# Hybrid layer with retrieved experts on one core: gathers of four choices of 32 tokens, 128x32 products, and another order of the head

## The reference

```
mod = silu(c) @ w_ada + b_ada                  # shift1, scale1, gate1, shift2, scale2, gate2
h = rms_norm(x, g_norm1) * (1 + scale1) + shift1
a, u, v = split(h @ w_in)                      # three times 512 columns
mixed = concat(pool_mixer(a), u * spatial(layer_norm(v)))   # windows of 2..16; 128-token chunks
x = x + gate1 * (mixed @ w_out)
h = rms_norm(x, g_norm2) * (1 + scale2) + shift2
q = h @ w_query                                # 8 heads x 2 sides x 128
scores = q . sub_keys                          # 128 keys a side
s_top, i_top = top_k(scores, 16)               # each side
best, sel = top_k(s_top0[:, None] + s_top1[None, :], 16)
idx = 128 * i0 + i1                            # one of 16384 experts
gate = softmax(best)
act = gelu(expert_down[idx] . h)
x = x + gate2 * sum(gate * act * expert_up[idx])
out = rms_norm(x, g_final)
```

## Time and profile before

| | us |
|---|---|
| median of 3 runs | 2961.24 (2958.83 to 2965.78) |
| the profiled execution's own time | 2958.65 |
| its span, first to last instruction | 2956.9 |
| TensorE busy | 2140.7 (72%) |
| VectorE busy | 1882.0 (64%) |
| ScalarE busy | 1144.8 (39%) |
| POOL busy | 1117.3 (38%) |
| moved by DMA | 1158.09 MB, mean 392 GB/s |
| mean granted TensorE clock | 0.797 of full speed |

### The profile page before, as it was taken

The page is one execution under the profiler, slowest core; times in us unless marked ns, Lnnn a source line. Parts: engine busy times, 40 slices in busy tenths (PEclk is TensorE's granted clock), DMA queues, the critical chain, the costliest instruction groups (busy, mean ns, idle before and its releaser), DMA issues.

```text
span 2956.9 us, 35079 instructions
## 1 busy us (share of the span) xinstructions
PE 2140.7 (72%) x12226; PEld 790.5 (27%) x12226; DVE 1882.0 (64%) x4560; ACT 1144.8 (39%) x3504; POOL 1117.3 (38%) x1029
## 2 busy tenths in 40 slices
PE   4587797888977767776767777777666677767665
PEld 3353352343523222221122222222111222222210
DVE  3846655665565666666676666666666666666664
ACT  1124335354352334433343434343343434343333
POOL 0013333343332444433444444434444444444432
PEclk9698898998978687877687677777777777777776
DMA  9459999999999999999999999999999999999997
GB/s 404 161 195 384 348 356 409 373 410 386 348 399 368 410 421 421 421 410 421 421 416 421 411 419 409 422 408 421 420 407 421 409 420 405 421 411 419 421 421 299
DMA packets 162730, 1158.09 MB, mean 392 GB/s; under 512 B 18164, under 2 KB 18932, under 8 KB 28024
## 3 DMA queue, kind: packets, MB, share of 16 engines
q0 software_dynamic: 147456, 1073.81, 88.9%
q1 hardware_dynamic: 15096, 82.04, 7.2%
HBM read 1147.38 MB, written 8.39 MB: 391 GB/s over the span
## 4 chain that ended last, share of the span: by engine, by line
DMA 47%; PE 30%; DVE 11%; ACT 7%; issue 3%; POOL 1%; SPq 0%; DVEq 0%; ACTq 0%; POOLq 0%
DMA weights<-experts,expert_rows 25%; DMA work<-experts,expert_rows 22%; PE ps_sum L635 13%; PE ps_q L606 6%; PE ps_m L577 3%; DVE work L1099 3%; DVE weights L1099 3%; PE ps_m L524 2%; PE ps_m L546 2%; PE ps_m L537 2%; ACT diag L800 2%; ACT weight L795 1%; POOL work L464 1%; DVE wide L875 1%; ACT act_out L793 1%
## 5 line engine op out<-in xcount | busy, mean ns | idle before, releaser
L635 PE MATMUL ps_sum<-work,diag 64*64 64x512 f32 x6656 | 1176.0, 792 | 534.9 <-ACT diag L800 532.3
L1099 DVE CUSTOM_DVE_ANT_0 work<-work,h_cur 128x1024 f32<-128x1024 f32 x832 | 1017.6, 1224 | 712.0 <-DMA work<-experts,expert_rows 710.2
L464 POOL DMA_INDIRECT work<-experts,expert_rows x832 | 893.8, 1074 | 1474.7 <-PE ps_sum L635 1263.8
L793 ACT ACTIVATE act_out<-act_in 128x1 f32<-128x1 f32 x1024 | 207.3, 202 | 1346.2 <-DVE act_in L1099 1345.5
L635 PEld LDWEIGHTS ps_sum<-work,diag 64*64 64x64 f32 x6656 | 210.7, 158 | 1339.9 <-ACT diag L800 1273.5
L635 PE MATMUL ps_sum<-weights,diag 64*64 64x512 f32 x1536 | 308.4, 886 | 186.4 <-ACT diag L800 177.3
L800 ACT ACTIVATE diag<-const,weight 128x64 f32<-128x64 f32 x1024 | 356.0, 348 | 33.5
L464 POOL DMA_INDIRECT weights<-experts,expert_rows x192 | 223.1, 1162 | 334.3 <-PE ps_sum L635 321.2
L1099 DVE CUSTOM_DVE_ANT_0 weights<-weights,h_cur 128x1024 f32<-128x1024 f32 x192 | 234.8, 1223 | 147.5 <-DMA weights<-experts,expert_rows 147.5
L795 ACT ACTIVATE weight<-gate,act_out 128x1 f32<-128x1 f32 x1024 | 301.8, 295 | 33.2
L606 PEld LDWEIGHTS ps_q<-h_t,weights 128*128 128x128 f32 x1152 | 144.0, 203 | 69.3 <-issue 69.3
(11 more groups left out here) (149 smaller groups left out, 1390.1 us busy)
## 6 DMA issues: line engine op xcount, KB each, us to landing
work<-w_ada SPq DMA_DIRECT2D x12, 2048.0 KB, 15.2
work<-w_query SPq DMA_DIRECT2D x7, 2048.0 KB, 11.5
work<-experts,expert_rows POOLq DMA_INDIRECT x832, 15.3
weights<-w_in SPq DMA_DIRECT2D x3, 2048.0 KB, 16.8
weights<-w_query SPq DMA_DIRECT2D x3, 2048.0 KB, 18.1
x_buf<-x SPq DMA_DIRECT2D x8, 512.0 KB
weights<-w_out SPq DMA_DIRECT2D x2, 2048.0 KB, 31.3
x_scratch<-h_buf SPq DMA_DIRECT2D x8, 512.0 KB, 3.0
```

The source lines that it names most:

```text
L464: nc.gpsimd.indirect_dma_start(ring[r], None, experts, bass.IndirectOffsetOnAxis(ap=expert_rows[:, g % SLOTS:g % SLOTS + 1], axis=0),).the ...
L635: last = nc.tensor.matmul(ps_sum[n * ROWS:(n + 1) * ROWS, r, :], diag[rows, slot, :], ring[slot][rows, D + n * HALF:D + (n + 1) * HALF], s ...
L793: nc.scalar.activation(act_out[:, s:s + 1], act_in[:, s:s + 1], ACT.Gelu).then_inc(s_gelu, 1)
L1099: nc.vector.tensor_tensor_reduce(down, down, h2_cur[:, :], 1.0, 0.0, ALU.mult, ALU.add, act_in[:, g % TURN:g % TURN + 1]).then_inc(s_dots, 1)
```

## The change

**The gather.** A gather still fetches 128 rows of 8 KB, but they are four choices of 32 tokens, where they were one choice of 128 tokens. All four quarters of the partitions then belong to the same 32 tokens. `diag` is 128x32, and `add_expert` makes four products of 128x32, each streaming 256 columns. The tokens' `h2` must stand four times below each other for the dots: `spread_h2` (a product of 32 rows by 128x512, two a segment) and `copy_spread` on ScalarE do that for each segment of 8 slots (tile 0) or 16 slots (from tile 1), 72 segments in all. The choices must be moved to their partitions: a 19th route step, four small products (`move_choices`) and two copies (`place_choices`) a turn. `y`, `x1_fin`, `gate2` and `gf` are in quarters too, so `load_x1_final` and `store_out` move rows of 1 KB, 32 partitions at a time, four transfers where there were two.

**The weights of the queries.** They come in sides (a side is half a head, 128 partitions of 4608 bytes, 0.59 MB, query and key weights together) in a buffer of two. Tiles 0 to 2 stream every side; from tile 3 on three turns of four find theirs held in SBUF (12 sides, loaded at slot 257), and the first turn's four sides are streamed in each tile. `LOAD_OF` has 66 sides; with 2 that go to ring slots at first and the 12 held, 80 sides are loaded.

**The mixer's steps.** There are 35 steps, with the U and out projections cut into twice as many pieces. Tile 1's mixer has 22 of its steps in slots 0 to 21, where 7 of 31 were.

**The head.** GATE1's sum stands ahead of tile 0's layer norm; tile 0's out projection runs on unscaled `w_out` and VectorE multiplies the result by gate1; `w_out` is scaled after the first route. The bias rows are put into the sums' tiles at first, so no row is added at the end. The first query is done side by side.

The core of the diff:

```diff
+QUADS = 4
+QROWS = P // QUADS
...
-MIX_AT = {1: -MIX_HEAD, 2: 12, 3: 48, 4: 93, 5: SLOTS + 4, 6: SLOTS + 40, 7: SLOTS + 85}
...
+MIX_AT = {1: -MIX_HEAD, 2: 25, 3: 64, 4: 103, 5: 142, 6: 181, 7: 220}
...
+BATCHES = [((0,), (1,), (2,), (3,))] + [((0, 1), (2, 3))] * (TILES - 1)
...
+def streamed(e):
+
+    return e // PAIRS <= MIX_TILES or e % PAIRS == 0
...
+            def load_side(e, b):
+                n = LOAD_OF[e, b]
+                if n >= 2:
+                    before = [key for key, m in LOAD_OF.items() if m == n - 2][0]
+                    sp.wait_ge(s_score, 4 * before[0] + before[1] + 1)
+                sp.dma_start(side_buf[n % 2], sides[4 * (e % PAIRS) + b]).then_inc(s_side[n % 2], 16)
...
-                for n in range(2):
-                    sp.dma_start(x1_fin[n * ROWS:(n + 1) * ROWS, :, :], x1_rows[t, n]).then_inc(s_x1f, 16)
...
+                for c in range(QUADS):
+                    sp.dma_start(x1_fin[quarter(c), :, :], x1_rows[t, c]).then_inc(s_x1f, 16)
...
+            def spread_h2(k, half):
...
+                pe.wait_ge(s_wide_sb, use)
+                nc.tensor.matmul(ps_wide[:, :], quads[quarter(group), :],
+                                 source[quarter(group), half * HALF:(half + 1) * HALF],
+                                 start=True, stop=True).then_inc(s_wide_ps, 1)
...
+            def add_expert(x):
...
+                for c in range(QUADS):
+                    last = nc.tensor.matmul(ps_sum[quarter(c), x.group, :], diag[:, x.ring, :],
+                                            ring[x.ring][:, D + c * QCOLS:D + (c + 1) * QCOLS],
+                                            start=x.first, stop=x.last, skip_group_check=True)
                 last.then_inc(s_free, 1)
...
             norm2(0)
-            mixer(2, 1)
+            mixer(FACTOR1, 1)
             sum_ada(GATE2)
             for n in range(ROUTE_STEPS):
-                route_step(n, 0, 0)
-            for n in (13, 16, 21, 22, 23):
-                mixer(n, 1)
```

More of the change, by code:

```diff
@@ L387, in _ @@
[L387 to L388 removed]
+            sp.wait_ge(s_zero, 3)
+            for m in (GATE1, SHIFT2, SCALE2):
+                sp.dma_start(totals[m][0:1, :], b_ada[m * D:(m + 1) * D].unsqueeze(0)).then_inc(s_b_ada, 16)
             load_ada(GATE1, 0)
@@ new lines, in _ @@
+            mod_rows(SCALE2)
+            turn_h2(0, 0)
+            turn_h2(0, 1)
+            side(0, 0)
+            side(0, 1)
+            for b in range(4):
+                scores(0, b)
+                if b < 2:
+                    side(0, b + 2)
+            spread_h2(0, 0)
+            spread_h2(0, 1)
+            mixer(TURN_H, 1)
+            mod_rows(GATE2)
+            move_choices(0)
+            for b in range(4):
+                side(1, b)
+                scores(1, b)
+            for n in range(TURN_H + 1, MIX_HEAD):
+                mixer(n, 1)
```

1136 lines of the change are left out of this document (628 added, 508 removed).

## The result

The changed kernel takes 2978.97 us, median of 6 runs (2973.78 to 2988.84); the kernel before took 2959.80 in the 6 runs beside it. The ratio is 1.0070, 95% interval 1.0048 to 1.0091: slower by 0.7%. The prediction said 2973, within 2938 to 3006. The profiled execution took 2976.63 us with a span of 2974.8, so 17.9 us more span than before.

What follows compares the result with a forecast made beforehand. The kernel was taken as a DMA transfer of 1158.09 MB at 421 GB/s plus 206 us of unused bandwidth. Terms +56 + 18 - 16 - 47 + 1 gave +12 us: 2973, range 2938 to 3006.

Steps and rivals of the forecast that it cites:

- Item 1: Query and key weights: 80 sides, 47.2 MB, replace 23.6 MB, so 23.6 MB more at 421 GB/s, +56 us.
- Item 2: Reads of x1 in 1 KB rows: cost goes by the row, +18 us after slot 256 and +6 before.
- The stated bound of 0: Other bound for the x1 reads: the halved rows cost nothing.
- rival A: Faster: quarter reads of x1 are free, the dip coming from something other than row length; 2949 us, chance 0.25.
- Item 3: Head, to 225 us: unused bandwidth falls from 89 to 73 us, first refill at about 193.5; -16 us.
- Item 4: Tiles 0 and 1: unused bandwidth falls from 75 to 28 us, -47 us, the 6 for x1 reads included.
- Item 5: Later tiles keep their 33 us unused, plus 18 for x1 reads; spreads and moves lie beside; tail +1 us.
- rival C: Slower: the four 128x32 products do not run together, about 120 us more TensorE time, 3090 us; chance 0.04.
- D: Slower: the next tile's x1 arrives late and dots queue, 2 us in each of 6 tiles, 2985; within forecast's range.
- B: No change: forecast's mechanism, but tiles 0 and 1 lose only some 8 us beside the reads; 2962 us, chance 0.18.

Runs made afterwards that it cites:

- resident sides: Changed kernel with all 16 sides kept in SBUF from tile 2 on, 60 sides loaded instead of 80: 2959.40 us, ratio 0.9995 to the kernel before.
- The test that moved the sum: Changed kernel with GATE2's sum ahead of tile 1's first mixer factor on VectorE instead of behind it: 2972.49 us, ratio 1.0043 to the kernel before.
- The one tried: Changed kernel with U in four steps of eight products and the eight out steps spread over slots 21 to 31: 2993.23 us, ratio 1.0106 to the kernel before.

## Why the prediction was right, and where it was not

**Bound.** Right: bytes at 421 GB/s, and bandwidth not used by stage. The changed kernel adds up in this form to 2 us.

**Item 1, bytes +56.** Right: 56.4 from the bytes. By place tile 2 grew by 31 us (about 30 forecast), and resident sides took 25 of 28 back by the trace and 20 by the medians.

**Item 2, x1 in 1 KB rows, +18 and +6.** Wrong. The step that failed is "If the cost goes by the row, 512 rows cost 6.0". The row measured one length only. With two more lengths the loss is the same 1.6 to 1.9 us for 1 KB and for 2 KB rows, and none for one read of 4 KB rows into all partitions. The stated bound of 0 was right, and the prediction's own sign of being wrong, dips of x1 no larger, came; rival A held in the later tiles: tiles 3 to 6 are 4.8 us longer on average, not 8. The Trainium skill ("DMA: Bandwidth & Descriptors", Specifications) gives 512 B as the least transfer for line rate. Halving from 2 KB was free, as that rule has it; but both lengths lose 1.6 to 1.9 us that the 4 KB read does not, and this the rule doesn't foresee.

**Item 3, the head, -16.** Right in mechanism and nearly in size: -13. Out projection at 75.60 (76), VectorE waiting 20.02 (20), first gather at 158.86 (161.5), V's norm at 185.83 (185), first refill at 193.81 (193.5). The test that moved the sum confirmed what sets the refill.

**Item 4, tiles 0 and 1, -47.** Too large: -27 in the profile, and by the scatter rather less. The step that failed is the 19 us taken for "waits of one engine for another with a ring of 6", a term that no row gave. Without the two dips of x1 (3 to 4 us) the measured term is 44 us. With it went "no stretch is over the DMA by more than 3.5 us". The sum counted an out slot as 3.0 us by spreading queries evenly. In the trace the eight out slots from 224.74 to 250.69 take 25.95 us, 3.24 each, since four halves of queries and two spreads (1.12 us) fall into them. The seven mixers' stretches of eight out slots take 21.9 to 28.9 us, 3.14 a slot on average, and that is 4 us over the DMA's 22 in three of them and 7 in one, which begins with tile 1. V slots were sized right, at 3.15 where 3.1 was counted. So the out slots were counted 8 us too short in all, and the greater part of the miss is in the term of the waits itself. Four V slots, and then the eight out slots of the same mixer (columns of the earlier trace rows):

```profile
393.76:405.91 12.15, 12.15 (x75) 6.03 (x75) 3.95 (x11) 4.67 (x17) 6.08 (x5) 1.00 1.01 420
456.75:482.68 25.93, 25.93 (x138) 11.27 (x137) 7.76 (x16) 6.97 (x26) 8.82 (x8) 0.99 0.87 312
```

TensorE works without a pause in both. The first is short and the DMA stays full, the second loses 6.7 us. The seven out stretches lose 22 of the 47.8 us, the V stretches 2, and 24 stand between them, in slots in which TensorE has pauses (over the two tiles it waits 118 us for ScalarE's `diag`). The low clock at the start of a stretch comes on top in some (a first step of 2.95 for 1.98 us at 590.83, a V step of 2.91 at 515.82). The runs size the parts by taking work away: by the medians 28 us hang on TensorE's V and out steps, 11 on VectorE's windows, means and gating and 12 on ScalarE's tables, each good to about 7. They are not to be added (the sum, 51, is more than the 47.8 lost), since each shortens the others' waits. The wait for the moved choices, which the prediction had hidden ("32 moves lie beside it"), is real at 45 us and costs nothing that could be measured.

**Item 5, tail and moves.** Right: +1, and later tiles otherwise as before.

**Signs and sums that do not fit one another.** The prediction puts the end of tile 1 near 900 us. Its own terms give 926: 981, and 8 of the bytes ahead of tile 2, less 16 and 47. Measured is 947, and item 4 is 20 of the difference. The upper ends of its items add to 3011 and not 3005, and rival C by its own slots (143 us of TensorE in 107, six mixers) is over 200 us and not 120. None of this moves the forecast.

**The rivals.** C did not come: eight products of 128x32 take 0.64 us at 2.4 GHz and 1.08 at 1.2, and not 2.0. D did not come: from tile 2 on VectorE waits for the next tile's x1 once, 8.2 us ahead of 1042.60, and tiles 3 to 6 stay under the forecast. B did not come: tiles 0 and 1 lose 44 us beside the reads, not 8. A was half right, in the x1 reads, and was outweighed by item 4. The close total is thus luck in part: item 2 was 19 us too dear from tile 2 on, and item 4 was 20 us too hopeful.

What stays open: whether the row's length or the partitions make the x1 read lose bandwidth, why the early part of tile 0 starts at either clock from one profile to another, and what a layout that leaves TensorE and VectorE no common dense stretch would give. The one tried was worse.

## What to carry to other kernels

When a kernel is a transfer with holes, price a change in two separate accounts, bytes at the full rate and bandwidth left unused by stage: the first came out here within 3 us of the trace. For the second, lay the real steps of every engine into the real slots, and ask how long a dense stretch is: TensorE without a pause for 12 us cost nothing here, for 26 us up to 7. Where three engines wait for one another, as in the tiles with mixers, cutting any one of them gained something and none gained all. A cost that was measured at one size has no slope: measure a second size before you scale it.
